# Latent attention: the causal mask added by VectorE in its pass for the row maximum, in place of a mask product on TensorE

## The chip, the core and the metric

The kernel runs on one core of a Trainium2 chip. Five engines run side by side and meet at semaphores: TensorE (PE in the rows; its weight loads are PEld), VectorE (DVE), ScalarE (ACT), GpSimd (POOL) and SyncE (SP), which here only issues transfers. TensorE writes its products to PSUM ("banks", eight per core); everything else lies in SBUF (one big tensor called "arena"). The metric is the device time of one execution in microseconds. Three executions of the kernel before took 2721.03, 2726.42 and 2727.64 us; their median is 2726.42.

## The reference

The program is two blocks of a language model over 1024 tokens of width 1024 in float32: a layer with latent and sliding-window attention, a layer of attention with forget gates, a mixer, cross attention and a mixture of experts. The change lies in the latent attention of the first layer alone:

```
def causal_block_attention(q, k, v, log_cum=None):     # 8 heads here, Dk = 96, Dv = 64
    scale = Dk ** -0.5
    def one_block(i):                                  # 128 queries at a time
        s = einsum('bqhd,bkhd->bhqk', qi, k) * scale
        ...
        mask = kpos[None, :] <= qpos[:, None]
        s = where(mask, s, -inf)
        p = softmax(s, axis=-1)
        return einsum('bhqk,bkhd->bqhd', p, v)
```

## The kernel before

Each engine has a program of its own, written out in full by Python loops; the order of the instructions on an engine is the order of the code, and nothing reorders it. The latent attention is the part between `queries` and the sliding-window attention (`swa`). Its 8 heads are taken in 4 pairs, and each pair in 8 steps of 128 queries: step s = 0 to 31 has pair s // 8 and block t = s % 8, and works on n = 128 (t + 1) keys for each of two heads, h = 0 and 1. I call "step t" of a pair the one with that t. Pair 3 is the last one.

What one step has on each engine (`Pairs`, `pe_pairs`, `act_pairs`, `dve_pairs`, lines 579 to 721):

- TensorE, `pe_mla_scores` (line 816): for h = 0, then h = 1, the score product of n columns into two banks (2h, 2h + 1) of PSUM, cut at 512 columns. The profile shows each float32 product as two passes. Behind each head's product a bf16 product of a unit matrix and the mask table (`identb`, `maskq`) adds -1e30 above the diagonal of the last 128 columns. The banks of head h are free for this once the exponential of the step before has read them. In steps t = 1 and t = 5 the weighted values of the four steps before follow (`values`, bank 6). Then come the transposes of the weights of step s - 1, head 0 (`pe_turn`, line 173 in the rows), a filler (a projection for the next pair: line 170, 8 or more products of 128 columns; pair 3 has none), and the transposes of head 1. They go through banks 4 and 5 in turn, four blocks at a time, so for t >= 4 a head takes both.
- VectorE, `dve_mla_largest` (line 854): the negated row maximum of head 0 and of head 1 out of PSUM (line 858), then for step s - 1 the reciprocal of the sums (line 700), the product of the gates and that (line 705), in steps t = 1 and 5 the product of the weighted values and the gates (line 712), its share of the copies out of banks 4 and 5 (line 716), and the gate of the filler (line 734).
- ScalarE, `act_mla_exponentials` (line 838): for each head exp(score - maximum), read from PSUM, written to one of three buffers `PM` in turn, with the row sums beside it (line 845). Then its share of the copies of step s - 1, head 0 (line 682), the filler's part, and the copies of head 1 (line 686).

A buffer `PM[(2s + h) % 3]` may be written again once the transposes of its last contents are done: for head 1 of step s these are the transposes of head 0 of step s - 1, which TensorE makes behind the scores of step s. In the kernel before ScalarE has this wait (`mla.turned(C, ...)`), ahead of its exponential. In the block with t >= 4 the first bank that head 1's transposes need is the one that ScalarE empties at line 682.

The forget-gate attention further on (`fox`, lines 1338 to 1424) has the same classes and loops. There VectorE already adds a row to the scores in its pass for the maximum and writes them to memory, and ScalarE reads them there (lines 1400 and 1377). It has four buffers.

## Time and profile before

| | |
|---|---|
| median of three executions | 2726.42 us (2721.03 to 2727.64) |
| span of the profiled execution, first to last instruction | 2725.1 us |
| TensorE busy | 2560.0 us, 94% |
| VectorE, ScalarE, GpSimd busy | 944.5, 594.3, 118.0 us |
| mean granted TensorE clock | 0.973 |
| latent attention, first maximum to its last product by the gates | 133.4 to 337.9 us |

The page gives one number for the profiled execution, its span of 2725.1 us; that is 1.3 us under the median of the timed ones, which themselves lie 6.6 us apart. "Busy" of TensorE includes pipelined ends of products, so 94% doesn't say that 6% is all there is to gain. In a row of the timeline the first number is the start in us from the start of the span, the second the busy time of the group, and in brackets stand the idle time of that engine before it and what ended that idle time.

### The profile page before, as it was taken

The numbers are of one execution on the slowest core, as the hardware profiler recorded it, in microseconds if no ns is written. First come the engines' busy times: TensorE is split into PE (matmuls) and PEld (weight loads), VectorE is DVE, ScalarE is ACT, GpSimd is POOL, SyncE is SP. The second block draws the span as 40 slices with busy tenths as digits, with TensorE's granted clock in tenths as the row PEclk, the third lists the DMA queues.
The fourth block names the chain that finished last, engine by engine and source line by source line (L and its number), as shares of the span: only waits on it lengthen the run. The fifth ranks groups of instructions, "written<-read, shape, count | busy, mean of one in ns | idle before, by whom it ended". The sixth has DMA issues, their size and how long they took to land. (4 is left out here: it accounts for less than half of the span.)

```text
span 2725.1 us, 27911 instructions
## 1 busy us (share of the span) xinstructions
PE 2560.0 (94%) x11166; PEld 1617.1 (59%) x11166; DVE 944.5 (35%) x2421; ACT 594.3 (22%) x1466; POOL 118.0 (4%) x140
## 2 busy tenths in 40 slices
PE   8899899999999999999899999999999999699992
PEld 5676466644666556665544666644554765487771
DVE  4344424512122222222412566663300243521115
ACT  3344323401132222322401211110000210011111
POOL 1000000000000000000000000000000000012112
PEclk9999999999999999999999999999999999699996
DMA  4000110222200111101051300004150122438876
GB/s 155 1 1 1 56 54 1 64 92 71 63 19 28 47 47 47 41 6 47 32 140 55 96 5 32 31 1 162 54 185 0 62 99 105 139 97 268 267 229 190
DMA packets 146951, 210.35 MB, mean 77 GB/s; under 512 B 17008, under 2 KB 101872, under 8 KB 146816
## 3 DMA queue, kind: packets, MB, share of 16 engines
q1 hardware_dynamic: 139904, 183.33, 20.5%
q0 software_dynamic: 6912, 25.17, 3.9%
q8 instruction: 91, 1.49, 0.2%
q14 instruction: 44, 0.36, 0.0%
HBM read 170.66 MB, written 37.81 MB: 77 GB/s over the span
## 5 line engine op out<-in xcount | busy, mean ns | idle before, releaser
L170 PE MATMUL banks<-arena 128*128 128x512 f32 (+13 forms) x9038 | 2349.2, 440 | 52.5 <-ACT arena L1036 8.8
L170 PEld LDWEIGHTS banks<-arena 128*128 128x128 f32 (+4 forms) x9038 | 1393.2, 186 | 892.3 <-issue 776.4
L173 PE MATMUL banks<-arena 128*128 128x128 f32 (+1 forms) x1936 | 284.4, 281 | 63.4 <-ACT arena L682 18.1
L173 PEld LDWEIGHTS banks<-arena 128*128 128x128 f32 (+1 forms) x1936 | 227.3, 144 | 130.5 <-issue 68.3
L1400 DVE CUSTOM_DVE_ANT_0 arena<-arena,banks 128x256 f32<-128x256 f32 (+7 forms) x128 | 91.4, 751 | 191.2 <-PE banks L170 191.1
L252 POOL TENSOR_TENSOR arena<-arena 128x1 f32<-128x1 f32 (+1 forms) x88 | 56.7, 646 | 2321.8 <-DVE arena L1186 1410.6
L716 DVE COPY arena<-banks 128x128 f32<-128x128 f32 (+3 forms) x144 | 70.2, 487 | 207.6 <-PE banks L173 207.6
L1377 ACT ACTIVATE arena<-arena 128x256 f32<-128x256 f32 (+7 forms) x128 | 98.2, 768 | 106.0 <-DVE arena L1400 106.0
L1181 DVE TENSOR_TENSOR arena<-arena,banks 128x1024 f32<-128x1024 f32 x16 | 19.5, 1221 | 167.1 <-PE banks L170 167.1
L1155 ACT ACTIVATE arena<-banks 128x512 f32<-128x512 f32 x32 | 18.8, 588 | 266.2 <-PE banks L173 266.2
L2058 DVE SCALAR_TENSOR_TENSOR arena<-arena,banks 128x1024 f32<-128x1024 f32 x16 | 19.5, 1221 | 149.6 <-PE banks L170 149.6
L845 ACT ACTIVATE arena<-banks,arena 128x128 f32<-128x128 f32 (+7 forms) x64 | 47.4, 740 | 82.2 <-DVE arena L858 54.7
L1169 ACT ACTIVATE arena<-arena 128x1024 f32<-128x1024 f32 x16 | 16.9, 1057 | 218.6 <-DVE arena L1181 218.6
L1321 ACT ACTIVATE arena<-banks 128x512 f32<-128x512 f32 x32 | 19.1, 597 | 207.5 <-PE banks L170 207.5
L858 DVE TENSOR_REDUCE arena<-banks 128x1 f32<-128x128 f32 (+7 forms) x64 | 48.1, 756 | 30.4 <-PE banks L170 30.0
L2287 DVE TENSOR_REDUCE arena<-banks 128x4 f32<-128x1024 f32 x8 | 9.8, 1224 | 131.9 <-PE banks L170 131.9
L686 ACT ACTIVATE arena<-banks 128x512 f32<-128x512 f32 (+2 forms) x96 | 49.6, 517 | 19.4 <-PE banks L173 19.2
L1058 DVE SCALAR_TENSOR_TENSOR arena<-arena,banks 128x256 f32<-128x256 f32 (+1 forms) x64 | 22.8, 398 | 86.4 <-PE banks L170 86.4
L2604 POOL DMA_INDIRECT x_scratch<-arena,places x24 | 37.8, 1577 | 213.8 <-DVE arena L2755 213.8
L1326 ACT ACTIVATE arena<-banks 128x256 f32<-128x256 f32 x32 | 12.3, 383 | 154.5 <-PE banks L170 154.5
L1025 ACT ACTIVATE arena<-arena 128x256 f32<-128x256 f32 (+1 forms) x64 | 31.1, 487 | 55.9 <-DVE arena L1067 55.9
L2755 DVE TENSOR_SCALAR arena<-banks,arena 128x512 f32<-128x512 f32 x24 | 18.0, 751 | 66.7 <-PE banks L170 66.7
(269 smaller groups left out, 1164.5 us busy)
## 6 DMA issues: line engine op xcount, KB each, us to landing
x_scratch<-arena SPq DMA_DIRECT2D x40, 512.0 KB, 2.8
arena<-in_o_w_in_dram SPq DMA_DIRECT2D x32, 512.0 KB, 6.6
arena<-x_scratch SPq DMA_DIRECT2D x32, 512.0 KB, 5.3
arena<-in_w_gate_dram SPq DMA_DIRECT2D x16, 1024.0 KB, 15.2
arena<-in_w_up_dram SPq DMA_DIRECT2D x16, 1024.0 KB, 17.4
arena<-in_w_down_dram SPq DMA_DIRECT2D x16, 1024.0 KB, 8.7
arena<-in_x_dram SPq DMA_DIRECT2D x16, 512.0 KB, 4.9
arena<-decay_scratch SPq DMA_DIRECT2D x16, 512.0 KB, 6.3
```

The source lines that it names most:

```text
L170: return pe.matmul(o, a, b, start=start, stop=stop)
L173: return pe.transpose(o, a, ident)
L252: return pool.tensor_tensor(y, v, mhalf[:, 0:v.shape[1]], ALU.pow)
L686: act.activation(dst, src, ACT.Copy).then_inc(pt_a.sem, 1)
L716: vec.tensor_copy(dst, src).then_inc(pt_v.sem, 1)
L845: act.activation(mla.weights(s, h)[:, 0:n], bank(2 * h, 2)[:, 0:n], ACT.Exp, bias=a8[:, h:h + 1], accum_out=a8[:, 2 + h:3 + h]).then_inc(e ...
L858: vec.tensor_reduce(a8[:, h:h + 1], bank(2 * h, 2)[:, 0:n], AXX, MAX, negate=True).then_inc(mx_done.sem, 1)
L1025: act.activation(sw3[:, h, lo:256], sw3[:, h, lo:256], ACT.Exp, bias=a8[:, h:h + 1], accum_out=a8[:, 4 + h:5 + h])
L1058: m = vec.scalar_tensor_tensor(sw3[:, h, lo:256], DM[:, lo:256], -2.0 ** -(2 * p + h + 1), sc[:, 512 * h + lo:512 * h + 256], MUL, ADD)
L1377: act.activation(w, w, ACT.Exp, bias=a8[:, h:h + 1], scale=-1.0, accum_out=a8[:, 2 + h:3 + h]).then_inc(ex_done.sem, 1)
L1400: vec.tensor_tensor_reduce(fox.weights(s, h)[:, 0:n], NB[p % 2][:, h, 0:n], bank(2 * h, 2)[:, 0:n], 1.0, BIG, ADD, MIN, a8[:, h:h + 1]).th ...
L2604: pool.indirect_dma_start(out=x5, out_offset=bass.IndirectOffsetOnAxis(ap=PUT[:, c:c + 1].bitcast(U32), axis=0), in_=YS[i % 3], in_offset= ...
```

## The change

VectorE's pass changes from a maximum (`tensor_reduce`) to a `tensor_tensor_reduce`: it adds a table `MLM` (896 zero columns and the 128 columns of the mask, of which the last n are taken) to the scores in PSUM, writes the sum to the step's `PM` buffer, and takes its row minimum. For this the queries are scaled by -MSC, so the stored values are the negated scores, and the exponential takes scale=-1. The exponential now works in place in SBUF. The mask products on TensorE go; the scores wait for the row maxima of the step before (`mx_done`) where they waited for its exponentials. The wait for the transposes moves from ScalarE to VectorE. `MLM` takes 1024 words in a weight buffer (`w1`), so the transposed gates move to another place in it, and the keys' weights of the sliding-window attention land in its other half. Two instructions that fill `MLM` come ahead of VectorE's first gate.

```diff
-        w_skv = tiled(weights("keys of swa", 1, 1)[:, 0:2048], 8)
+        w_skv = tiled(weights("keys of swa", 1, 1)[:, 2048:4096], 8)
...
-                        act.activation(qt[:, 384 * n:384 * n + 384], sb[:, 512 * n:512 * n + 384], ACT.Copy, scale=MSC)
+                        act.activation(qt[:, 384 * n:384 * n + 384], sb[:, 512 * n:512 * n + 384], ACT.Copy, scale=-MSC)
...
+        MLM = w1[:, 0:1024]
...
-                    tiled(XB[2][:, 512:1024], 4), w1[:, 2560:3072])
+                    tiled(XB[2][:, 512:1024], 4), w1[:, 1024:1536])
...
             for h in range(2):
-                P.wait_ge(ex_done, mla.ex + 2 * s - 1 + h)
+                P.wait_ge(mx_done, mla.mx + 2 * s - 1 + h)
...
-                    mm(sc[:, b:b + w], QT8[0:96, 2 * p + h, 128 * t:128 * t + 128], KA[2 * (p % 2) + h][0:96, b:b + w], True,
-                       b + w != n)
-                mm(sc[:, n - 128:n], identb[:, :], maskq[:, :], False, True).then_inc(s_done.sem, 1)
+                    m = mm(sc[:, b:b + w], QT8[0:96, 2 * p + h, 128 * t:128 * t + 128], KA[2 * (p % 2) + h][0:96, b:b + w], True,
+                           True)
+                m.then_inc(s_done.sem, 1)
...
                 C.wait_ge(mx_done, mla.mx + 2 * s + h + 1)
-                if 2 * s + h >= 3:
-                    i, h_ = divmod(2 * s + h - 3, 2)
-                    mla.turned(C, ("p", i, h_, i % 8 // 4))
-                act.activation(mla.weights(s, h)[:, 0:n], bank(2 * h, 2)[:, 0:n], ACT.Exp, bias=a8[:, h:h + 1],
+                w = mla.weights(s, h)[:, 0:n]
+                act.activation(w, w, ACT.Exp, bias=a8[:, h:h + 1], scale=-1.0,
                                accum_out=a8[:, 2 + h:3 + h]).then_inc(ex_done.sem, 1)
...
                 V.wait_ge(s_done, mla.s + 2 * s + h + 1)
-                vec.tensor_reduce(a8[:, h:h + 1], bank(2 * h, 2)[:, 0:n], AXX, MAX, negate=True).then_inc(mx_done.sem, 1)
+                if 2 * s + h >= 3:
+                    i, h_ = divmod(2 * s + h - 3, 2)
+                    mla.turned(V, ("p", i, h_, i % 8 // 4))
+
+                vec.tensor_tensor_reduce(mla.weights(s, h)[:, 0:n], MLM[:, 1024 - n:1024], bank(2 * h, 2)[:, 0:n], 1.0, BIG,
+                                         ADD, MIN, a8[:, h:h + 1]).then_inc(mx_done.sem, 1)
...
+            vec.memset(MLM[:, 0:896], 0.0)
+            vs(vec.tensor_scalar(MLM[:, 896:1024], CST[:, C_MQ:C_MQ + 128], -1.0, None, MUL))
+            vs.done()
```

VectorE in step t = 5 of the first pair, before. The rows are the two maxima (line 858), then the reciprocal, the gates, the product by the gates and the copies of step s - 1; "scores", "weights_turned" and "exponentials" are the events of line 574 and 575.

```order
L858 TENSOR_REDUCE arena<-banks 128x1 [waits scores] x2
L700 RECIPROCAL arena<-arena 128x2 [waits exponentials]
L705 TENSOR_TENSOR arena<-arena 128x128 [waits vector_step,gate_ready]
L712 TENSOR_TENSOR arena<-banks,arena 128x512 [waits turned_weights_by_dve,weighted_values]
L716 COPY arena<-banks 128x128 [waits weights_turned] x2
```

The same step of the same engine now. Line 861 is the new pass; the row of 128x1 behind it reads its minimum out.

```order
L861 ISA arena<-arena,banks 128x768 [waits scores]
L861 ISA arena 128x1
L861 ISA arena<-arena,banks 128x768 [waits weights_turned,scores]
L861 ISA arena 128x1
L700 RECIPROCAL arena<-arena 128x2 [waits exponentials]
L705 TENSOR_TENSOR arena<-arena 128x128 [waits vector_step,gate_ready]
L712 TENSOR_TENSOR arena<-banks,arena 128x512 [waits turned_weights_by_dve,weighted_values]
L716 COPY arena<-banks 128x128
L716 COPY arena<-banks 128x128 [waits weights_turned]
```

The wait for "weights_turned" now stands ahead of the second pass, and all that follows it in VectorE's queue is behind it. TensorE in step t = 7 of pair 3 (s = 31), first before, from the scores to the transposes of head 0 of the step before it:

```order
L170 MATMUL banks<-arena 128x512 [waits exponentials]
L170 MATMUL banks<-arena 128x512
L170 MATMUL banks<-maskq,identb 128x128
L170 MATMUL banks<-arena 128x512 [waits exponentials]
L170 MATMUL banks<-arena 128x512
L170 MATMUL banks<-maskq,identb 128x128
L173 MATMUL banks<-arena 128x128 [waits turned_weights_by_act]
L173 MATMUL banks<-arena 128x128 x3
L173 MATMUL banks<-arena 128x128 [waits turned_weights_by_dve]
L173 MATMUL banks<-arena 128x128 x2
```

and now:

```order
L170 MATMUL banks<-arena 128x512 [waits row_max]
L170 MATMUL banks<-arena 128x512
L170 MATMUL banks<-arena 128x512 [waits row_max]
L170 MATMUL banks<-arena 128x512
L173 MATMUL banks<-arena 128x128 [waits turned_weights_by_act,exponentials]
L173 MATMUL banks<-arena 128x128 x3
L173 MATMUL banks<-arena 128x128 [waits turned_weights_by_dve]
L173 MATMUL banks<-arena 128x128 x2
```

Two products go, and the wait for the exponentials stands at the transposes. ScalarE in step t = 5 of the first pair, before (line 845 the exponentials, 682 the copy of head 0, 730 the filler's gate, 686 the copy of head 1) and the exponentials of step t = 6:

```order
L845 ACTIVATE arena<-banks,arena 128x768 [waits row_max]
L845 ACTIVATE arena<-banks,arena 128x768 [waits weights_turned,row_max]
L682 ACTIVATE arena<-banks 128x4x128 [waits weighted_values]
L730 ACTIVATE arena<-banks 128x128 [waits gate_ready,filler_projected]
L686 ACTIVATE arena<-banks 128x4x128 [waits weights_turned]
L845 ACTIVATE arena<-banks,arena 128x896 [waits weights_turned,row_max] x2
```

and now:

```order
L844 ACTIVATE arena<-arena 128x768 [waits row_max] x2
L682 ACTIVATE arena<-banks 128x4x128 [waits weighted_values,weights_turned]
L730 ACTIVATE arena<-banks 128x128 [waits gate_ready,filler_projected]
L686 ACTIVATE arena<-banks 128x4x128 [waits weights_turned]
L844 ACTIVATE arena<-arena 128x896 [waits row_max] x2
```

The exponential of head 1 has lost its wait for the transposes, and the copy behind it has taken one. No engine's other instructions change places, and no transfer is issued at another place in its queue.

## Rows read from the trace of the kernel before

**Rows 1.** The page: engine shares, and the chain that ended last by line.

```profile
PE 2560.0 (94%) x11166; PEld 1617.1 (59%) x11166; DVE 944.5 (35%) x2421; ACT 594.3 (22%) x1466; POOL 118.0 (4%) x140
...
PE banks L170 27%; PE banks L173 2%; DVE arena L2045 0%; DVE arena L2885 0%; DVE arena L2883 0%; DMA x_scratch<-arena,places 0%; DVE arena L2688 0%; DMA arena<-x_scratch,slots 0%; DMA arena<-x_scratch 0%; DVE arena L2058 0%; DVE arena L2047 0%; DVE arena L2311 0%; DVE arena L2305 0%; ACT arena L2242 0%; DVE arena L2478 0%
```

**Rows 2.** Stretches: length, PE, PEld, DVE, ACT, POOL busy, clock, DMA share, GB/s.

```profile
180.00:230.00 50.00, 48.82 (x309) 34.00 (x308) 23.37 (x55) 22.84 (x55) 0.00 (x0) 1.00 0.00 1
...
280.00:330.00 50.00, 40.84 (x209) 24.36 (x208) 23.98 (x52) 20.74 (x48) 0.00 (x0) 0.93 0.19 63
```

**Rows 3.** Timeline of TensorE, step t = 7 of pair 2 (s = 23).

```profile
272.46 1.88 PE L170 MATMUL banks<-arena 96*128 96x512 f32 x4
274.18 0.22 PE L170 MATMUL banks<-maskq,identb 128*128 128x128 bf16 x1
274.24 1.93 PE L170 MATMUL banks<-arena 96*128 96x512 f32 x4
276.01 0.22 PE L170 MATMUL banks<-maskq,identb 128*128 128x128 bf16 x1
276.07 0.93 PE L173 MATMUL banks<-arena 128*128 128x128 f32 x7
...
279.28 0.98 PE L173 MATMUL banks<-arena 128*128 128x128 f32 x7 [0.48 <-ACT arena L682]
```

**Rows 4.** The same step: timeline of VectorE and of ScalarE, head 1.

```profile
276.27 1.23 DVE L858 TENSOR_REDUCE arena<-banks 128x1 f32<-128x1024 f32 x1 [0.61 <-PE banks L170]
...
277.53 1.11 ACT L845 ACTIVATE arena<-banks,arena 128x1024 f32<-128x1024 f32 x1 [0.63 <-DVE arena L858]
...
278.64 0.59 ACT L682 ACTIVATE arena<-banks 128x512 f32<-128x512 f32 x1
```

**Rows 5.** Timeline, step t = 5 of pair 2 (s = 21), behind the weighted values.

```profile
262.61 0.77 PE L173 MATMUL banks<-arena 128*128 128x128 f32 x5
...
263.48 0.90 ACT L845 ACTIVATE arena<-banks,arena 128x768 f32<-128x768 f32 x1 [2.48 <-PE banks L173]
...
264.37 0.59 ACT L682 ACTIVATE arena<-banks 128x512 f32<-128x512 f32 x1
...
265.01 0.76 PE L173 MATMUL banks<-arena 128*128 128x128 f32 x5
```

**Rows 6.** Timeline, step t = 6 of pair 2 (s = 22).

```profile
268.79 0.82 PE L173 MATMUL banks<-arena 128*128 128x128 f32 x6
...
268.99 1.09 DVE L858 TENSOR_REDUCE arena<-banks 128x1 f32<-128x896 f32 x1 [0.52 <-PE banks L170]
...
271.75 0.87 PE L173 MATMUL banks<-arena 128*128 128x128 f32 x6 [0.35 <-ACT arena L682]
```

**Rows 7.** Timeline of the last step of the forget-gate attention, with the fused pass.

```profile
1354.50 1.22 DVE L1400 CUSTOM_DVE_ANT_0 arena<-arena,banks 128x1024 f32<-128x1024 f32 x1 [3.33 <-PE banks L170]
...
1355.77 1.15 ACT L1377 ACTIVATE arena<-arena 128x1024 f32<-128x1024 f32 x1 [4.64 <-DVE arena L1400]
...
1356.91 1.14 ACT L1377 ACTIVATE arena<-arena 128x1024 f32<-128x1024 f32 x1
...
1358.06 0.57 ACT L682 ACTIVATE arena<-banks 128x512 f32<-128x512 f32 x1
```

**Rows 8.** Timeline of TensorE in pair 3: head 1's transposes, steps t = 5 and t = 6.

```profile
309.59 0.77 PE L173 MATMUL banks<-arena 128*128 128x128 f32 x5 [1.63 <-ACT arena L682]
...
316.33 0.88 PE L173 MATMUL banks<-arena 128*128 128x128 f32 x3 [2.14 <-ACT arena L682]
```

**Rows 9.** Stretches at the lower clock (columns as in rows 2).

```profile
316.40:319.80 3.40, 3.40 (x9) 2.26 (x10) 0.42 (x1) 0.60 (x1) 0.00 (x0) 0.50 0.02 5
...
1350.70:1354.00 3.30, 3.30 (x9) 1.12 (x8) 0.42 (x1) 0.43 (x1) 0.00 (x0) 0.50 0.00 0
```

**Rows 10.** A fill of 1024 columns by VectorE, and VectorE's first gate.

```profile
L1756 DVE MEMSET arena<- 128x1024 f32 x1 | 0.9, 912 | 0.2 <-issue 0.2
...
120.73 0.49 DVE L734 SCALAR_TENSOR_TENSOR arena<-arena,banks 128x128 f32<-128x128 f32 x2 [1.85 <-ACT arena L730]
```

## Prediction, made before the changed kernel was run

> **What bounds the kernel now.** I read the page first: TensorE is busy 94% of the span, and the chain that ended last runs almost wholly over its products [rows 1]. The change touches one stage, the latent attention, so I cut that into stretches. In the pairs that have fillers TensorE is busy 48.82 of 50 us at the full clock, VectorE and ScalarE under half of it; in the stretch with most of pair 3, which has none, TensorE has 40.84 of 50 us and a mean clock of 0.93 [rows 2]. So for three pairs TensorE's own work sets the time, and what it waits for in pair 3 sets the rest. Then I read the timeline of single steps, since the pairs repeat to the hundredth: what does TensorE wait for where it waits? In steps t = 6 and t = 7 it is always ScalarE's copy of line 682, 0.35 and 0.48 us [rows 3, 6]; in step t = 5 the copy comes just in time [rows 5]; in pair 3 the same wait is 1.63 us in step 5 and 2.14 in step 6 [rows 8].
>
> The chain behind that wait is what the reader is to see. In step t = 7: TensorE ends the scores of head 1 with a mask product at 276.01; VectorE's maximum starts at 276.27; ScalarE's exponential at 277.53; its copy at 278.64, which stands behind it in its queue; TensorE's transposes of head 1 at 279.28, that is 0.64 us behind the start of the copy [rows 3, 4]. None of these waits for the transposes of head 0 that TensorE makes from 276.07 on: the buffer is ScalarE's to wait for, and it is free (276.07 + 0.93 = 277.00) before the maximum is ready.
>
> **The change, part by part.**
>
> *Mask products.* A mask product holds TensorE for 0.06 us, from its start to that of the next product (274.18 to 274.24, 276.01 to 276.07). The scores behind the first one also lose something: four passes of 512 columns take 274.24 to 276.01 = 1.77 us there, and 272.46 to 274.18 = 1.72 us ahead of it [rows 3]. I take the 0.05 as a weight load that a product of 128 columns is too short to hide. A step so saves 0.06 + 0.05 + 0.06 = 0.17 us; 32 steps, 5.4 us in all if TensorE's work set every one. The bounds are 3.8 us (64 x 0.06) and 5.4.
>
> *VectorE's pass.* The trace has the fused pass in the forget-gate attention: 1.22 us for 1024 columns, against 1.23 for the plain maximum [rows 4, 7]. The exponential starts 1.27 us behind it (1354.50 to 1355.77), 1.26 behind the old one (276.27 to 277.53). So the pass itself costs nothing. It is also the same instruction, with the same kind of operands; I take no bound wider than 0 to 0.1 us each.
>
> *The exponential out of SBUF.* From its start to the copy behind it: 1.15 us (1356.91 to 1358.06) against 1.11 (277.53 to 278.64) [rows 4, 7], 0.04 more. It counts only in the steps whose chain ends at the copy.
>
> The Trainium skill says in "VectorE: DVE Perf Modes", section "The TRN2 errata", that ScalarE pays a fixed 224 cycles for an operand in SBUF and 172 out of PSUM; that is 52 cycles at 1.2 GHz, an estimate of 0.043 us, and the trace agrees with its 0.04. The same table gives VectorE less for SBUF (58 cycles) than for PSUM (120); a pass that reads both should gain nothing by it, and the two rows of 1.22 and 1.23 us bear that out. By that page the sum stays as it is.
>
> *The wait that moves.* This is the term that decides. VectorE's pass of head 1 now writes the buffer, so it must wait for the transposes of head 0 of the step before, which TensorE makes behind the scores of this step. The maximum used to run beside them. What is queued behind the waiting pass: on VectorE the reciprocal, the gates, its copies; behind the event, ScalarE's exponential and the copy of line 682, for which TensorE waits. What each step loses, with the 0.17 us taken off where TensorE gets to the transposes sooner:
>
> - t = 7: the transposes end at 277.00 - 0.17 = 276.83; VectorE starts some 0.04 us later, 276.87 in place of 276.27: 0.60 late. With the exponential's 0.04, TensorE goes on 0.65 us later than 279.28.
> - t = 6: they end at 268.79 + 0.82 - 0.17 = 269.44; the pass starts at 269.48, not 268.99: 0.49, and 0.53 at the copy. TensorE already waited here, so all of it counts [rows 6].
> - t = 5: the weighted values lie between scores and transposes, so before, the maximum was long done and ScalarE waited for the transposes (2.48 us). They end at 262.61 + 0.77 - 0.17 = 263.21. Now the pass of 768 columns comes between: about 0.96 us from its start to its end (1.09 for 896 and 1.22 for 1024 give 0.13 for each 128), 0.05 to the exponential: 264.25, where it was 263.48; the copy 0.80 late, and so TensorE, whose 265.01 was on the edge [rows 5].
> - t = 0 to 4: the filler (16 products, about 1.95 us by its place between 263.21 and 265.01 in step 5) or the one bank per head covers the delay; nothing is lost and 5 x 0.17 = 0.87 us is saved.
>
> A pair with fillers: 0.65 + 0.53 + 0.80 - 0.87 = +1.1 us. Three of them: +3.3.
>
> Pair 3 has no filler. Steps 5, 6 and 7 lose the same 1.98 us, since TensorE waits for the copy in each [rows 8]. In step 0 the loss is small (the pass over 128 columns is short): +0.14. Steps 1 to 4 have a second effect: scores wait for the maxima, not for the exponentials, so they can start sooner, but VectorE's queue is held by its wait. Bounds for the four: -0.7 (all mask products saved) less what the earlier start gives, and +0.3 a step if VectorE's wait ends them. I take -0.5. Pair 3: +1.6.
>
> *The start.* Two fills of the table, 896 and 128 columns; 1024 columns take 0.912 us, and VectorE is idle for 1.85 us ahead of its first gate, while ScalarE loads a table [rows 10]. About 1.2 us of fills go into it. Cover gone, it would cost under 1.2 us. The moved weights are issued at the same point, behind the last filler, into memory that is free by then: nothing.
>
> **Sum:** 3.3 + 1.6 = +4.9 us on the profiled span of 2725.1; the median of the timed runs, 2726.4, is 1.3 us over that span, and 4.9 us on it give 2731.3, that is +0.18%. A measurement of this kernel can tell about 0.3% (8.2 us) from no change, so this is "no change that can be told", on the slow side.
>
> **Rivals.**
>
> *The delay is hidden and the mask products are pure gain.* TensorE then saves 5.4 us: 2721.0. For it: TensorE is the bound, the scores' banks come free one exponential sooner, and the fused pass in the forget-gate attention does no harm. Against it: there the transposes awaited lie two steps back, with four buffers; here it is one step, and the trace has no slack in t = 5, 6 and 7. It would need ScalarE's copy to be no part of TensorE's wait, which three rows deny [rows 3, 6, 8].
>
> *The longer idle times let TensorE's clock fall.* After the idle 2.14 us at 316.33 the clock is 0.50 for 3.4 us, 1.2 in place of 2.4 GHz, and the same happens in the forget-gate attention [rows 8, 9]; after the 1.63 us at 309.59 it did not. Now these waits grow to about 2.14 + 0.53 + 0.17 = 2.8 us in step 6 of pair 3 and 1.63 + 0.80 + 0.17 = 2.6 us in step 5. One more stretch costs at most half its length, 1.7 us, since its work is done at half speed. In the pairs with fillers the waits grow from 0, 0.35 and 0.48 to about 1.0, 1.05 and 1.3 us; if the clock fell there once a pair, that is 3 x 1.7 more. All four: 4.9 + 6.8 = +11.7, 2738.1, slower. It decides from an idle time between 1.63 and 2.14 us on if the rows here are the measure, so I expect it in step 5 of pair 3 at most (+1.7, inside my range), and not in the others.
>
> *The two terms cancel.* If VectorE's pass reacts sooner, or the steps 1 to 4 of pair 3 gain from the earlier scores as much as TensorE can use (some 0.5 us a step, -2 in place of -0.5), and the chain in step 5 is shorter than I walked it, the sum is near +1: 2727.5.
>
> **How the numbers follow.** Forecast, +3 to +7 us: 0.50. Cancel: 0.15. Hidden, pure gain: 0.13. Clock or another wait that makes it +8 or more: 0.22. Faster by over 0.3% needs more than all the mask products are worth, so it is noise on the second case alone: 0.04. Slower by over 0.3% is nearly all of the clock case and a tenth of the forecast: 0.26. The rest, 0.70, is within 0.3%. The range takes in the pure gain but for its far side and the clock case but for its far side: 2721 to 2738. The likeliest case alone would span 2729 to 2735. I give its middle with a little of the clock's 1.7 us, 2731.5.
>
> **What would show it right or wrong.** In the profile after: VectorE's pass of head 1 starts 0.04 us behind the transposes of head 0 in every step with t >= 2, and ScalarE has no wait for transposes left ahead of its exponentials. TensorE's waits for line 682 in a pair with fillers read about 1.0, 1.05 and 1.3 us in t = 5, 6, 7. The stage, 204.5 us from its first maximum to its last product by the gates, becomes 209.4; if it becomes shorter than 204.5, the moved wait is covered and I am wrong in the main term. Pair 3 is 1.6 us longer, or 3.3 with one more stretch at 0.50. A fused pass longer than 1.3 us for 1024 columns, or a VectorE gate later than 120.73, would be a cost that I put at nothing.

## The result, and the profile after

| | before | after |
|---|---|---|
| first comparison, median of four executions each | 2725.92 us (2721.03 to 2727.64) | 2740.2 us (2731.83 to 2743.76) |
| second comparison (`e1_after_again`) | 2726.46 us (17 executions) | 2737.02 us (2730.86 to 2744.32, 6 executions) |
| span of the profiled execution | 2725.1 us | 2730.4 us |
| latent attention, first pass for the maximum to the last product by the gates | 204.54 us | 211.91 us |

The changed kernel is slower: ratio 1.0048 [1.0036, 1.0061] in the first comparison, 1.0049 [1.0034, 1.0064] in the second, some 11 to 14 us. I had forecast +4.9 us, a median of 2731.5 and a range up to 2738: the first median lies past it, the second (2737.02) just inside. One thing has to be said of these numbers before they can be read: executions of the changed kernel differ by 13 us among each other, those of the kernel before by 7 in the first comparison and by 10 in the second (2718.11 to 2728.39), and the profiled one of the changed kernel was the fastest of its four. So a single profile doesn't tell this kernel's time, and I look at six of them below.

First the page, whose lines answer to [rows 1]. Each group of part 5: busy, mean ns of one | idle time ahead of it, and what ended most of it.

```profile
PE 2551.9 (93%) x11102; PEld 1612.0 (59%) x11102; DVE 945.2 (35%) x2487; ACT 596.0 (22%) x1466; POOL 118.3 (4%) x140
...
L173 PE MATMUL banks<-arena 128*128 128x128 f32 (+1 forms) x1936 | 284.0, 281 | 76.9 <-ACT arena L682 30.4
...
L861 DVE CUSTOM_DVE_ANT_0 arena<-arena,banks 128x128 f32<-128x128 f32 (+7 forms) x64 | 48.1, 753 | 67.4 <-PE banks L173 50.8
...
L844 ACT ACTIVATE arena<-arena 128x128 f32<-128x128 f32 (+7 forms) x64 | 49.6, 775 | 93.4 <-DVE arena L861 93.3
```

TensorE has 64 products fewer (11166 to 11102) and is busy 8.1 us less, yet the span is longer: the time went into waiting. The two other lines say where the wait now is. VectorE's new pass waits for transposes (L173), 50.8 us in sum, and ScalarE's exponential for nothing but that pass; over the whole program TensorE's transposes wait 30.4 us for the copy of line 682, where it was 18.1.

The stretches, for [rows 2]:

```profile
180.00:230.00 50.00, 46.56 (x283) 32.15 (x282) 22.56 (x64) 22.25 (x53) 0.00 (x0) 1.00 0.00 1
...
280.00:330.00 50.00, 37.30 (x201) 22.35 (x199) 23.13 (x67) 21.50 (x48) 0.00 (x0) 1.00 0.19 63
```

TensorE's busy time in 50 us of a pair with fillers fell from 48.82 to 46.56 us, at the full clock in both. So these pairs are longer by waits, not by the clock. In the last stretch it fell from 40.84 to 37.30, here with a clock of 1.00 where it was 0.93; part of that fall is the clock, since the same product is busy for longer at the lower one.

The step t = 7 of pair 2, for [rows 3, 4]; start, busy time, and in brackets the idle time before:

```profile
278.78 1.22 DVE L861 CUSTOM_DVE_ANT_0 arena<-arena,banks 128x1024 f32<-128x1024 f32 x1 [1.10 <-PE banks L170]
...
280.30 0.93 PE L173 MATMUL banks<-arena 128*128 128x128 f32 x7
...
281.38 1.22 DVE L861 CUSTOM_DVE_ANT_0 arena<-arena,banks 128x1024 f32<-128x1024 f32 x1 [1.36 <-PE banks L173]
282.52 0.08 DVE L861 DVE_READ_ACCUMULATOR2_ANT arena<- 128x1 f32 x1
...
282.64 1.15 ACT L844 ACTIVATE arena<-arena 128x1024 f32<-128x1024 f32 x1 [1.35 <-DVE arena L861]
...
283.79 0.58 ACT L682 ACTIVATE arena<-banks 128x512 f32<-128x512 f32 x1
...
284.51 0.74 PE L173 MATMUL banks<-arena 128*128 128x128 f32 x5 [1.49 <-ACT arena L682]
```

Follow it downward: transposes of head 0, pass of head 1, exponential, copy, transposes of head 1. It is the chain that I had walked. Two of its links are longer than I took them. The pass starts at 281.38, 0.15 us behind the end of the transposes (280.30 + 0.93 = 281.23), where I took 0.04. TensorE goes on 0.72 us behind the start of the copy (283.79 to 284.51), where it was 0.64 [rows 3, 4]. The other two are as read: 1.26 us from pass to exponential, 1.15 to the copy. TensorE waits 1.49 us here, not 1.3.

Steps t = 5 and t = 6 of the same pair, for [rows 5, 6]:

```profile
265.18 0.77 PE L173 MATMUL banks<-arena 128*128 128x128 f32 x5
265.78 1.95 PE L170 MATMUL banks<-arena 128*128 128x128 f32 x16
266.09 0.95 DVE L861 CUSTOM_DVE_ANT_0 arena<-arena,banks 128x768 f32<-128x768 f32 x1 [3.44 <-PE banks L173]
...
268.74 0.74 PE L173 MATMUL banks<-arena 128*128 128x128 f32 x5 [1.01 <-ACT arena L682]
...
272.32 0.82 PE L173 MATMUL banks<-arena 128*128 128x128 f32 x6
...
273.29 1.09 DVE L861 CUSTOM_DVE_ANT_0 arena<-arena,banks 128x896 f32<-128x896 f32 x1 [1.17 <-PE banks L173]
...
276.18 0.84 PE L173 MATMUL banks<-arena 128*128 128x128 f32 x6 [1.25 <-ACT arena L682]
```

The pass is again 0.14 and 0.15 us behind the transposes, and the waits are 1.01 and 1.25 us where I had 1.0 and 1.05.

And pair 3, for [rows 8]:

```profile
316.30 0.73 PE L173 MATMUL banks<-arena 128*128 128x128 f32 x5 [2.80 <-ACT arena L682]
...
323.74 0.85 PE L173 MATMUL banks<-arena 128*128 128x128 f32 x6 [3.04 <-ACT arena L682]
...
332.06 4.26 PE L173 MATMUL banks<-arena 128*128 128x128 f32 x19 [3.28 <-ACT arena L682]
```

The Trainium skill has a rule for the first of these links, in "Perfetto Trace Analysis", section "Per-engine timelines": the end that a profile gives for a matmul is computed, and only behind it does PSUM acknowledge and the semaphore reach the other engines. The 0.14 to 0.15 us agree with it; my 0.04 came from a single product of 128 columns behind which the maximum stood.

### The profile page after: what moved, and what is told of

Same layout as the page of the kernel before. It is cut to its first block and busy times, and to the rows that moved or that the text cites. A ratio compares the mean times of both kernels' runs of the same rounds, so it can differ in the third digit from the quotient of the medians.

```text
span 2730.4 us, 27907 instructions
## 1 busy us (share of the span) xinstructions
PE 2551.9 (93%) x11102; PEld 1612.0 (59%) x11102; DVE 945.2 (35%) x2487; ACT 596.0 (22%) x1466; POOL 118.3 (4%) x140
## 5 line engine op out<-in xcount | busy, mean ns | idle before, releaser
L173 PE MATMUL banks<-arena 128*128 128x128 f32 (+1 forms) x1936 | 284.0, 281 | 76.9 <-ACT arena L682 30.4
L173 PEld LDWEIGHTS banks<-arena 128*128 128x128 f32 (+1 forms) x1936 | 228.1, 143 | 147.4 <-issue 69.7
L861 DVE CUSTOM_DVE_ANT_0 arena<-arena,banks 128x128 f32<-128x128 f32 (+7 forms) x64 | 48.1, 753 | 67.4 <-PE banks L173 50.8
L844 ACT ACTIVATE arena<-arena 128x128 f32<-128x128 f32 (+7 forms) x64 | 49.6, 775 | 93.4 <-DVE arena L861 93.3
L2611 POOL DMA_INDIRECT x_scratch<-arena,places x24 | 37.9, 1578 | 213.5 <-DVE arena L2762 213.5
```

Of the source, the lines that this page charges most:

```text
L173: return pe.transpose(o, a, ident)
L844: act.activation(w, w, ACT.Exp, bias=a8[:, h:h + 1], scale=-1.0, accum_out=a8[:, 2 + h:3 + h]).then_inc(ex_done.sem, 1)
L861: vec.tensor_tensor_reduce(mla.weights(s, h)[:, 0:n], MLM[:, 1024 - n:1024], bank(2 * h, 2)[:, 0:n], 1.0, BIG, ADD, MIN, a8[:, h:h + 1]).t ...
L2611: pool.indirect_dma_start(out=x5, out_offset=bass.IndirectOffsetOnAxis(ap=PUT[:, c:c + 1].bitcast(U32), axis=0), in_=YS[i % 3], in_offset= ...
```

## Where the time lies: six profiles of the changed kernel

The pairs with fillers repeat in all six profiles to 0.02 us. From its first pass to that of the next, pair 1 and pair 2 take 53.84 us each, where they took 51.88 before; pair 0 takes 45.80 us, where it took 43.82. All that varies in the stage is pair 3, and it varies with the number of stretches of about 3.4 us that TensorE spends at a granted clock of 0.50 there:

| execution | such stretches in pair 3 | the stage, us | span, us |
|---|---|---|---|
| before | 2 | 204.54 | 2725.1 |
| after, first profile | 1 | 211.91 | 2730.4 |
| `e1_after_again` | 2 | 213.53 | 2729.5 |
| `e8_after_look` | 2 | 213.60 | 2732.9 |
| `e10_after_look` | 2 | 213.49 | 2733.4 |
| `e11_after_look` | 3 | 215.10 | 2735.7 |
| `e12_after_look` | 5 | 218.02 | 2739.5 |

From one stretch to five the stage grows by 6.11 us, 1.53 each. At an equal number (two) the change costs 213.5 - 204.5 = +9.0 us: 3 x 1.96 = 5.9 in the pairs with fillers and 3.1 in pair 3. (The kernel before has one profile only, so its two stretches are one sample.) The rest of the program varies too: span less stage is 2516.0 to 2521.5 us in the six profiles, 2520.6 in the one before. So the first profile of the changed kernel, with its +5.3 us, was near my +4.9 by luck: it had one stretch fewer in pair 3 than the kernel before, and 2.1 us less outside the stage.

The window from 300 to 350 us shows it in one row each (columns as in rows 2; the clock is the third number from the end): the first profile, then `e12_after_look`.

```profile
300.00:350.00 50.00, 37.66 (x172) 21.44 (x172) 19.63 (x50) 17.69 (x36) 0.00 (x0) 0.97 0.10 34
```

```profile
300.00:350.00 50.00, 38.03 (x156) 22.09 (x158) 19.56 (x52) 17.85 (x36) 0.00 (x0) 0.83 0.00 1
```

Mean clock 0.97 and 0.83, for the same program. The timeline of TensorE in `e12_after_look`:

```profile
317.13 1.30 PE L173 MATMUL banks<-arena 128*128 128x128 f32 x5 [2.80 <-ACT arena L682]
318.23 5.79 PE L170 MATMUL banks<-arena 96*128 96x512 f32 x8
...
327.71 1.51 PE L173 MATMUL banks<-arena 128*128 128x128 f32 x6 [3.04 <-ACT arena L682]
329.02 5.94 PE L170 MATMUL banks<-arena 96*128 96x512 f32 x8
```

The waits are the same as in the first profile to the hundredth, 2.80 and 3.04 us. There the five transposes behind the first of them took 0.73 us; here they take 1.30, at 1.2 GHz in place of 2.4, and the scores behind them 5.79 us for what takes 3.17 at the full clock. The same wait is followed by the lower clock in one execution and not in the next. And a long wait isn't needed: in `e6_copy_first` (below) the clock is 0.50 from 305.2 to 308.7 us, where TensorE had waited 0.67 and 1.14 us, and in `e2_wait_only` from 293.8 to 297.3 us, where it had waited 1.43 and 0.34 us, in step 0 of pair 3. So these runs give no length of a wait that decides it:

```profile
303.09 0.63 PE L173 MATMUL banks<-arena 128*128 128x128 f32 x4 [0.67 <-ACT arena L848]
304.86 0.33 PE L173 MATMUL banks<-arena 128*128 128x128 f32 x1 [1.14 <-DVE arena L716]
```

```profile
291.90 1.09 PE L173 MATMUL banks<-arena 128*128 128x128 f32 x8 [1.43 <-ACT arena L682]
293.34 0.63 PE L173 MATMUL banks<-arena 128*128 128x128 f32 x4 [0.34 <-ACT arena L686]
```

## The experiments

**The change once more.** `e1_after_again` is the changed kernel, for more executions.

> The changed kernel, unaltered, to see how its executions spread. Theory A (moved wait plus clock): the moved wait alone makes the span 2730.4 us, as in the profiled execution with a mean granted clock of 0.975; executions at a lower mean clock are longer, about 12 us for 0.005 less, so spans lie between 2730 and 2743 and fall on one line with the clock. Rival B (the extra time of the timed runs has nothing to do with TensorE's clock, for instance transfers): spans of 2735 to 2743 come at the same mean clock as 2730.

Measured: 2737.02 us against 2726.46, ratio 1.0049. The slowdown stands. Its executions took 2730.86 us at a mean clock of 0.976, 2736.75 at 0.973, 2744.32 at 0.970: the line of theory A, not rival B.

**The moved wait alone.** `e2_wait_only` is the kernel before, mask products and all, with the wait for the transposes put ahead of VectorE's plain maximum.

```diff
             for h in range(2):
                 V.wait_ge(s_done, mla.s + 2 * s + h + 1)
+                if 2 * s + h >= 3:
+                    i, h_ = divmod(2 * s + h - 3, 2)
+                    mla.turned(V, ("p", i, h_, i % 8 // 4))
```

> The kernel before with one wait more: VectorE's maximum of head h also waits for the transposes for which ScalarE waits; masks stay on TensorE, the maximum stays a plain reduction. Theory A: in steps t = 5, 6, 7 the maximum of head 1 starts 1.04, 0.77 and 0.88 us later (by the rows of before and 0.15 us from the transposes to VectorE), all of it in TensorE's wait: 2.7 us a pair, +10.8 us, about 2737, and more where the clock falls. Rival C (the fused pass or the exponential out of SBUF is what costs): no change, 2726.

Measured: 2745.3 us, ratio 1.0067 [1.0052, 1.0083]; a pair with fillers is 2.7 us longer, as expected (pair 2 takes 54.56 us). The whole is 19 us slower and not 11: its profile has five stretches at 0.50 in pair 3, three more than the kernel before, and the time outside the stage differs by 2 us besides. So in the pairs with fillers the wait is the whole loss and more, and the rest of the change gives some of it back. Its timeline in step t = 7:

```profile
283.95 0.93 PE L173 MATMUL banks<-arena 128*128 128x128 f32 x7
...
284.98 1.23 DVE L861 TENSOR_REDUCE arena<-banks 128x1 f32<-128x1024 f32 x1 [1.44 <-PE banks L173]
...
286.24 1.11 ACT L845 ACTIVATE arena<-banks,arena 128x1024 f32<-128x1024 f32 x1 [1.46 <-DVE arena L861]
...
287.35 0.59 ACT L682 ACTIVATE arena<-banks 128x512 f32<-128x512 f32 x1
...
287.99 0.98 PE L173 MATMUL banks<-arena 128*128 128x128 f32 x7 [1.32 <-ACT arena L682]
```

From transposes to transposes 4.04 us (283.95 to 287.99), against 4.21 in the changed kernel (280.30 to 284.51). The changed kernel's chain is 0.17 us longer: 0.05 ahead of the pass, 0.04 in the exponential, 0.08 behind the copy's start. That is as much as its mask products save in a step. In the three steps where this chain sets the time, taking the mask products away therefore brought next to nothing: steps t = 5, 6 and 7 take 9.33, 7.76 and 7.39 us in the changed kernel, 9.36, 7.80 and 7.36 here.

**The mask products alone.** `e3_no_mask` is the kernel before without them. It leaves the causal mask out, so its weights and all that follows differ; with these data the expert part further on takes another branch (its page has 128 passes of a loop at lines 2820 to 2841 that the kernel before never enters), and the whole time (4942 us) compares with nothing. Apart from the mask products the latent attention itself issues the same instructions, and can be read.

```diff
-                mm(sc[:, n - 128:n], identb[:, :], maskq[:, :], False, True).then_inc(s_done.sem, 1)
+                m.then_inc(s_done.sem, 1)
```

> The kernel before without the mask products, and nothing in their place (the latent attention is computed without its causal mask; the work is otherwise the same). Theory A: each step is 0.17 us shorter, on TensorE's work as well as on the chain through VectorE and ScalarE: -5.4 us, 2720.5. Rival D (the mask products were hidden in waits): -2 us or less.

Measured: the stage takes 198.27 us, not 204.54, with one stretch at 0.50 and not two, so that some 4.7 of the 6.3 us are the mask products (1.53 us for the stretch). A pair takes 50.63, -1.25, which is 0.16 a step on average (0.10 to 0.18). My 0.17 a step stands. Of the measured +1.96 of a pair, +2.69 is the wait and -1.25 the mask products; what is left is +0.52. By steps, t = 5, 6 and 7 have 0.43 of it, 0.13 to 0.15 each, about the 0.17 of the longer chain that I walked in t = 7; the rest lies in t = 0 and t = 4.

**The other way to keep the sum.** `e4_back_to_psum` is the changed kernel, but VectorE writes the masked scores back to the banks they came from. The exponential reads them there and writes `PM`, so the wait is ScalarE's again, and the scores wait for the exponentials.

```diff
-                P.wait_ge(mx_done, mla.mx + 2 * s - 1 + h)
+                P.wait_ge(ex_done, mla.ex + 2 * s - 1 + h)
...
-                vec.tensor_tensor_reduce(mla.weights(s, h)[:, 0:n], MLM[:, 1024 - n:1024], bank(2 * h, 2)[:, 0:n], 1.0, BIG,
+                vec.tensor_tensor_reduce(bank(2 * h, 2)[:, 0:n], MLM[:, 1024 - n:1024], bank(2 * h, 2)[:, 0:n], 1.0, BIG,
```

> The changed kernel, but the fused pass writes the masked, negated scores back into their banks of PSUM; the exponential reads them there, writes the buffer and has the wait for the transposes again, and the scores wait for the exponentials again. So masks are off TensorE and the wait isn't moved. Theory A: as e3, -5.4 us, 2720.5. Rival C (the fused pass costs): slower than e3 by what the pass costs, up to 2731. If the pass is slower because it writes to PSUM, its rows show it.

Measured: 2722.25 us (2716.11 to 2723.11), ratio 0.9981 [0.9973, 0.999]; a pair 50.75 us. Same arithmetic, same mask table, no mask products, and faster than before, by 4.2 us where I had expected 5.4; the stage is 200.68 us, 3.9 shorter, with two stretches at 0.50 as before. Step t = 7:

```profile
272.04 0.93 PE L173 MATMUL banks<-arena 128*128 128x128 f32 x7
...
272.24 1.23 DVE L859 CUSTOM_DVE_ANT_0 banks<-arena,banks 128x1024 f32<-128x1024 f32 x1 [0.43 <-PE banks L170]
...
273.39 0.14 DVE L859 DVE_READ_ACCUMULATOR2_ANT arena<- 128x1 f32 x1
...
273.56 1.11 ACT L846 ACTIVATE arena<-banks,arena 128x1024 f32<-128x1024 f32 x1 [0.51 <-DVE arena L859]
...
274.67 0.59 ACT L682 ACTIVATE arena<-banks 128x512 f32<-128x512 f32 x1
...
275.31 0.98 PE L173 MATMUL banks<-arena 128*128 128x128 f32 x7 [0.55 <-ACT arena L682]
```

The pass (272.24) runs beside the transposes (272.04 to 272.97), and TensorE waits 0.55 us, not 1.49. The pass itself costs what the plain maximum does, to PSUM as to SBUF.

**The waits kept, but filled.** `e5_busy` is the changed kernel with products that nobody reads in TensorE's waits of steps t = 6 and 7 (in pair 3 t = 5, 6 and 7), ahead of the transposes of head 1.

```diff
+                if st is mla and s < st.n and s % 8 >= (5 if s >= 24 else 6):
+                    pe_mla_busy(s)
...
+            for _ in range(k):      # k = 4; in pair 3 k = 9 + (s % 8 - 5)
+                mm(bank(b)[:, 0:128], QT8[0:96, 0, 0:128], QT8[0:96, 1, 0:128], True, True)
```

> The changed kernel with products of 128 columns that nobody reads put ahead of TensorE's wait for the transposes of head 1: four (about 0.87 us) in t = 6 and 7 of pairs 0 to 2, nine to eleven (2.0 to 2.4 us) in t = 5, 6, 7 of pair 3; all shorter than the wait they stand in. Theory A (the spread and a part of the loss are TensorE's clock, which falls after these waits): the products cost nothing, the clock holds, every execution comes near the shortest of e1 (2731), median 2729 to 2733, mean clock 0.976 or more. Rival B (the loss beyond the profiled 2730 isn't the clock): median stays at 2737 or rises.

Measured: 2733.26 us (2730.15 to 2734.24, 11 executions), ratio 1.0027 [1.0017, 1.0036]. A pair still takes 53.84 us: the work lies in idle time. In pair 3 the waits fell:

```profile
317.16 0.74 PE L173 MATMUL banks<-arena 128*128 128x128 f32 x5 [0.79 <-ACT arena L684]
...
324.60 0.85 PE L173 MATMUL banks<-arena 128*128 128x128 f32 x6 [0.80 <-ACT arena L684]
```

```profile
300.00:350.00 50.00, 43.60 (x236) 27.42 (x237) 20.29 (x53) 17.85 (x36) 0.00 (x0) 1.00 0.11 37
```

The clock is 1.00 over the whole window and the stage takes 210.67 us with no stretch at 0.50; the changed kernel's 213.5 with two, less 2 x 1.53, would be 210.4. The executions spread over 4 us in place of 13; their median is at the upper edge of what I expected (2729 to 2733). This tells the two losses apart. Work that does nothing made the program faster, by 4 us against the median of `e1_after_again` and by 6 by the two ratios: that much of the 11 to 14 us went with the stretches. In the profile the chain is as long as it was, and the 7 us that remain fit it (the stage is 6.1 us longer than before, with two stretches fewer).

**Where the stretches lie.** `e8_after_look`, `e10_after_look`, `e11_after_look` and `e12_after_look` are the changed kernel, one profile each.

> The changed kernel once more, for another trace of the same program. Theory A: whatever its span, between 2729 and 2743 us, it is the 2730 of the profiled execution plus up to 1.7 us for each further stretch of low clock in the latent attention (or nearby), and those stretches begin behind one of TensorE's waits of 1.0 to 3.3 us.

> The changed kernel again, for one more trace. Open is where the low clock lies in executions of 2737 to 2744 us. Theory A: in the latent attention, behind waits of 1.0 to 1.5 us in pairs 0 to 2 (stage longer than 213.6 us). Rival G: elsewhere in the program (stage at 212 to 214 us whatever the span).

> As e10: one more trace of the changed kernel, with the same two expectations.

> As e10: one more trace of the changed kernel, with the same two expectations.

Measured: 2734.17, 2734.75, 2736.99 and 2740.78 us, and the table above. All stretches at 0.50 in the stage are in pair 3, none in pairs 0 to 2, whose waits are 1.01, 1.25 and 1.49 us. Of the difference between `e8_after_look` and `e12_after_look`, 6.6 us of span, pair 3 holds 4.4; the rest is outside the stage. So neither expectation of these runs came true as written: the stage does grow with the span, against rival G, but in pair 3 and not, as theory A had it, in pairs 0 to 2. None of the six profiles is of an execution above 2741 us, and 4 of the 14 executions of this kernel took 2743 to 2744 us: where those lose their time was not seen.

**The copy out of the chain.** If ScalarE's copy of step s - 1 is what TensorE waits for, and it only stands behind the second exponential because it was put there, then putting it between the two exponentials must cut the wait. `e6_copy_first` is the changed kernel with that order.

```diff
+                if h == 0 and s >= 1:      # behind the exponential of head 0
+                    for dst, src in turned_out(mla, C, s - 1, 0):
+                        act.activation(dst, src, ACT.Copy).then_inc(pt_a.sem, 1)
```

> The changed kernel with one change of order on ScalarE: the copies of head 0 of the step before stand between the exponentials of head 0 and head 1, not behind both. The wait on VectorE stays as the change put it. Theory A (the moved wait counts because the copy that TensorE needs is queued behind the delayed exponential): TensorE's waits for that copy (1.0, 1.25, 1.5 us in t = 5, 6, 7, up to 3.3 in pair 3) nearly go, some 0.2 us each stays for VectorE's own copy behind its pass: about -3.2 us a pair with fillers and -5 in pair 3, median about 2716. Rival E (the delay of VectorE's pass itself holds TensorE, by the scores' wait for the maxima): 2730 or more.

Measured: 2719.53 us (2717.56 to 2724.46), ratio 0.9976 [0.9966, 0.9987], a gain, though I had expected 2716. TensorE's waits in pairs 0 to 2 are 0.15 to 0.34 us, the stage 197.86 us. The moved wait is still there, and VectorE still has it, but in these pairs TensorE no longer waits behind the second exponential; 0.15 to 0.21 us are left for VectorE's own copy (line 716) behind its held pass. In pair 3 that copy still costs about 1 us in each of steps 5, 6 and 7.

**The order alone, and both.** `e9_before_copy_first` is the kernel before with that order; `e7_psum_copy_first` is `e4_back_to_psum` with it.

> The kernel before (masks on TensorE, plain maximum) with the order on ScalarE of e6 and e7: the copies of head 0 between the two exponentials. It tells how much of e7 is the order and how much the mask products. Theory A: the order alone takes the waits of 0.35 and 0.48 us in pairs 0 to 2 (-2.5 us in all) and most of 1.6, 2.1 and 2.3 us in pair 3 with a stretch of low clock (-5 to -6): about 2718 to 2720, and e7 (2712.5) is below it by the 5.4 us of the mask products. Rival F (the order only helps where the wait was moved): no change, 2726.

> e4 (masked scores back to PSUM, wait on ScalarE) with the same order on ScalarE as e6: the copies of head 0 between the two exponentials. Theory A: e4's waits for the copy go, 0.9 us a pair with fillers, some 5 us in pair 3: about 2714, the fastest so far.

Measured, both faster than expected: 2715.51 us for the order alone, ratio 0.9963 [0.9949, 0.9977], a pair 50.55 us, and 2712.51 us (2710.8 to 2713.18) for both, ratio 0.9949 [0.9936, 0.9963], a pair 49.28. The stage is 193.62 and 189.20 us. In `e7_psum_copy_first` step t = 7 reads:

```profile
268.49 0.93 PE L173 MATMUL banks<-arena 128*128 128x128 f32 x7
268.69 1.23 DVE L862 CUSTOM_DVE_ANT_0 banks<-arena,banks 128x1024 f32<-128x1024 f32 x1 [0.43 <-PE banks L170]
269.26 1.95 PE L170 MATMUL banks<-arena 128*128 128x128 f32 x16
...
269.40 0.59 ACT L850 ACTIVATE arena<-banks 128x512 f32<-128x512 f32 x1
...
270.02 1.11 ACT L846 ACTIVATE arena<-banks,arena 128x1024 f32<-128x1024 f32 x1
...
271.05 0.93 PE L173 MATMUL banks<-arena 128*128 128x128 f32 x7
```

The copy starts at 269.40, beside the filler, and TensorE goes from the filler (269.26 + 1.95 = 271.21) to the transposes without a wait; the start of 271.05 lies inside that, since the ends are modelled. This is the fastest version, 13.9 us under the 2726.36 us that the kernel before took beside it. The order alone gave 10.6 (against 2726.07). Not all of that is the shorter chain: neither profile has a stretch at 0.50 in the stage, where the kernel before has two, some 3 us. What taking the mask products away adds to the order, 3.0 us between the medians, is less certain, since the two intervals overlap; the stage is 4.4 us shorter in the profiles.

## Why the prediction was wrong

*Mask products, 0.17 us a step:* right (0.16 by `e3_no_mask`). *The fused pass, 0 to 0.1 us:* right, 1.22 us for 1024 columns. *The exponential, +0.04:* right, 1.15 us. *The start, nothing:* right; VectorE's first gate is at 120.02 us, 120.73 before.

*The moved wait.* The mechanism was right, and `e2_wait_only` shows it to be the whole loss: VectorE's pass behind the transposes, exponential and copy behind it, TensorE's wait at the end. Its size was not. The step that failed is "A pair with fillers: 0.65 + 0.53 + 0.80 - 0.87 = +1.1 us". Measured, from one first pass to the next (columns: growth of the step, and my term):

| | measured | predicted |
|---|---|---|
| t = 7 | +0.86 | +0.65 |
| t = 6 | +0.70 | +0.53 |
| t = 5 | +0.96 | +0.80 |
| t = 0 to 4 | -0.04, -0.16, -0.18, -0.17, -0.01 = -0.56 | -0.87 (5 x -0.17 is -0.85) |
| pair | +1.96 | +1.1 |

The three large steps are each 0.16 to 0.21 too small. The two mis-sized links explain it: 0.15 us, not 0.04, from the transposes to the pass, and 0.72, not 0.64, from the copy's start to TensorE, together 0.19. For the second there was a hint in the trace of before: in the forget-gate attention, whose exponential reads SBUF too, the copy starts at 1358.06 [rows 7], and the transposes behind it 0.72 us later (though at the lower clock, so the row alone proves nothing):

```profile
1358.78 1.09 PE L173 MATMUL banks<-arena 128*128 128x128 f32 x4 [3.48 <-ACT arena L682]
```

I took 0.64 from a step whose exponential reads PSUM.

And two of the five steps that I had as covered, t = 0 and t = 4, kept no gain. In t = 4 the profile shows why: VectorE's copy (line 716) stands behind the held pass, and the eight transposes take 1.21 us in place of 1.04:

```profile
257.68 0.82 DVE L861 CUSTOM_DVE_ANT_0 arena<-arena,banks 128x640 f32<-128x640 f32 x1 [0.80 <-PE banks L173]
...
258.90 0.69 DVE L716 COPY arena<-banks 128x512 f32<-128x512 f32 x1
...
259.16 1.21 PE L173 MATMUL banks<-arena 128*128 128x128 f32 x8
```

I had named those copies as queued behind the pass, and then costed only the exponential. For t = 0 the rows show where the gain stayed away, not why. From the start of the scores to the transposes of head 0 the changed kernel takes 232.07 - 231.46 = 0.61 us, the kernel before 228.84 - 228.22 = 0.62 with its two mask products, and `e3_no_mask` 227.23 - 226.70 = 0.53.

*Pair 3, +1.6:* at an equal number of slow stretches it is +3.1. Step 0 lost 0.43 (I had 0.14). Steps 1 to 4 gave +0.80, -0.46, -0.45, +0.13, that is 0.0, not -0.5; why step 1 lost 0.80 stays open. The other 2.6 are steps 5 to 7, where the 1.98 lacked three times the 0.19.

So the sum should have been +9.0 and not +4.9. That alone gives a median near 2735.4, inside the range: this step makes the size wrong by half, and the next one is needed to pass 2738.

*The clock.* The second step that failed is "so I expect it in step 5 of pair 3 at most (+1.7, inside my range), and not in the others". The rival that I rated at 0.22 came true in another shape. In the pairs with fillers the clock never fell, with waits up to 1.49 us; that half of my reasoning held. In pair 3 I treated the fall as an event that a wait's length decides, with one more at most. The six profiles have one to five of them behind waits that are the same to the hundredth, and the two stretches shown above, of `e6_copy_first` and `e2_wait_only`, follow waits of 1.14 and 1.43 us at most, under the 1.63 from which I had reckoned. The rival's 2738.1 lies close to the measured medians, but by other terms: it had the extra stretches in all four pairs and +4.9 for the chain. Against 9.0 at two stretches, the medians of +10.6 and +14.3 leave 2 to 5 us. At 1.53 each in pair 3 (I had 1.7 as the most) that would be one to three stretches more, which the profiles make likely and don't prove: the slowest executions have none, and the time outside the stage varies by as much. That the first median, of four executions, lay past 2738 and the second, of six, short of it is chance.

By the Trainium skill, "TensorE: Matmul & The Clock Gate", section "Terms", a penalty is the time at the reduced clock by the share of pulses dropped, half here: an estimate of 1.7 us for a stretch of 3.4. The profiles give 1.53, which fits with TensorE not being at work for all of each: in `e12_after_look` it was busy 5.99 of the 6.80 us from 326.9 on:

```profile
326.90:333.70 6.80, 5.99 (x12) 3.37 (x13) 1.45 (x2) 1.26 (x4) 0.00 (x0) 0.50 0.00 0
```

*The rivals.* "The delay is hidden" is out: `e2_wait_only` shows the wait's full price, +2.7 us a pair. "The terms cancel" is out as well. The other side, a faster kernel without mask products, exists, in these runs, where the wait goes back to ScalarE or the copy leaves the chain (`e4_back_to_psum`, `e6_copy_first`).

What stays open: why TensorE follows the copy by 0.72 us when the exponential ahead of it works in SBUF and by 0.64 when it reads PSUM, and what decides, in which execution and behind which wait, that the clock falls. That filling the waits ends it was shown for all of them together, not wait by wait.

## What to carry to other kernels

When a buffer's wait moves from one engine to the engine ahead of it in a chain, walk the whole chain, with links taken from rows of the same kind: a link behind a group of transposes is not one behind a single short product. Then ask what stands behind the chain's last instruction in its queue for no reason: here moving one copy between two exponentials was worth 10.6 us (some 3 of them two stretches of low clock that went with the waits), where all mask products together are worth about 5. And where a change lengthens TensorE's waits, count on a spread of executions and not on one profile: take several, and compare stretches at an equal clock.

## What the runs showed of the hardware

- A pass of VectorE that adds an SBUF table to 1024 columns of PSUM and takes the minimum costs 1.22 us with its sum written to SBUF and 1.23 to PSUM. The read of its accumulator behind it is 0.08 us in the first case and 0.14 in the second; from pass to exponential 1.26 us and 1.32.
- A VectorE pass held by transposes starts 0.14 to 0.15 us behind their modelled end in the changed kernel, 0.10 in `e2_wait_only`.
- The same waits of 2.8 to 3.3 us on TensorE were followed by between one and five stretches of 3.4 us at 1.2 GHz; waits up to 1.49 us between fillers by none, in six profiles of the changed kernel. In other versions, in pair 3, one such stretch came behind waits of 0.67 and 1.14 us (`e6_copy_first`) and one behind 1.43 and 0.34 us (`e2_wait_only`). Products that nobody reads, put into the long waits, kept 2.4 GHz through the stage in the one profile of that kernel, and shortened the program by 4 to 6 us.
